# Rotary embedding of the attention on VectorE in quarters of the partitions, and a sum of squares issued behind the cross attention's transposes

## The reference

```python
def _apply_rope(t, cos, sin):
    half = DIFF_HEAD_DIM // 2            # 32
    tf = t.astype(jnp.float32)
    t1, t2 = tf[..., :half], tf[..., half:]
    ...
    return jnp.concatenate([t1 * c - t2 * s, t1 * s + t2 * c], axis=-1)

q = _apply_rope(dq.reshape(Bsz, S, DIFF_HEADS, 2, DIFF_HEAD_DIM), cos, sin)
k = _apply_rope(dk.reshape(Bsz, S, DIFF_HEADS, 2, DIFF_HEAD_DIM), cos, sin)
v = dv.reshape(Bsz, S, DIFF_HEADS, 2 * DIFF_HEAD_DIM)
o = _diff_attention(q, k, v, lam)
o = _rmsnorm(o, diff_norm_w[layer]) * (1.0 - lambda_init)
y_diff = o.reshape(Bsz, S, DIFF_WIDTH) * jax.nn.silu(dg.astype(jnp.float32))
```

## Time and profile before

| what | value |
|---|---|
| median of 3 runs | 2605.24 us (2599.07 to 2606.93) |
| the profiled execution | 2600.93 us |
| its span, first to last instruction | 2599.1 us |
| TensorE products busy | 2454.3 us, 94% |
| VectorE busy | 1722.5 us, 66% |
| ScalarE busy | 1349.6 us, 52% |
| mean granted clock of TensorE | 0.986 of full speed |

### The profile page before, as it was taken

How to read it: one execution, slowest core, us unless ns; L and a number is a source line. 1 busy time by engine, 2 the same in 40 slices (tenths; PEclk the granted TensorE clock), 3 DMA queues, 4 the chain that set the end, 5 groups by cost and what they waited for, 6 DMA issues and landing times.

```text
span 2599.1 us, 51367 instructions
## 1 busy us (share of the span) xinstructions
PE 2454.3 (94%) x18962; PEld 2341.4 (90%) x18962; DVE 1722.5 (66%) x2571; ACT 1349.6 (52%) x2376; POOL 88.9 (3%) x96
## 2 busy tenths in 40 slices
PE   5898899999989989999999999999999999999998
PEld 4788799999978878999999999799999999889998
DVE  4677776666767776667576567577657656667655
ACT  4677655553457774555344444544445435555443
POOL 0000000000000000000010001001001001001000
PEclk9999999999989999999999999999999999999999
DMA  5344444445434444443545545344554554434553
GB/s 155 114 130 131 130 130 146 146 129 169 141 112 132 131 130 130 134 153 104 193 146 181 171 150 175 93 146 146 177 173 152 178 167 150 139 103 143 181 170 106
DMA packets 397711, 376.16 MB, mean 145 GB/s; under 512 B 27822, under 2 KB 396382, under 8 KB 397422
## 3 DMA queue, kind: packets, MB, share of 16 engines
q1 hardware_dynamic: 397550, 373.94, 45.5%
HBM read 372.84 MB, written 1.05 MB: 144 GB/s over the span
## 4 chain that ended last, share of the span: by engine, by line
PE 66%; issue 23%; DVE 5%; ACT 3%; POOLq 2%; DVEq 1%; DMA 1%; POOL 0%; SPq 0%; ACTq 0%
PE ps L501 18%; PE ps L503 18%; PE ps L502 18%; POOLq L466 1%; PE ps L715 1%; PE ps L716 1%; PE ps L717 1%; ACT scratch L960 1%; ACT w_hi L960 1%; DVE w_lo L1396 1%; DMA raw<-in_ffn_w_up 1%; PE ps L741 1%; DVE xT L1502 1%; PE ps L729 1%; PE ps L772 1%
## 5 line engine op out<-in xcount | busy, mean ns | idle before, releaser
L1396 DVE TENSOR_TENSOR w_lo<-raw,w_hi 128x1024 fp32r<-128x1024 f32 x704 | 860.7, 1229 | 471.4 <-ACT w_hi L960 469.3
L501 PE MATMUL ps<-x_hi,w_hi 128*128 128x272 f32 (+1 forms) x3648 | 1060.1, 291 | 22.3 <-DVE w_lo L1396 14.4
L502 PE MATMUL ps<-x_lo,w_hi 128*128 128x272 f32 (+1 forms) x3648 | 1043.8, 286 | 0.0
L503 PE MATMUL ps<-x_hi,w_lo 128*128 128x272 f32 (+1 forms) x3648 | 1042.2, 286 | 0.0
L960 ACT ACTIVATE w_hi<-raw 128x1024 fp32r<-128x1024 f32 x704 | 736.2, 1054 | 512.2 <-PE ps L503 358.3
L501 PEld LDWEIGHTS ps<-x_hi,w_hi 128*128 128x128 f32 x3648 | 690.9, 189 | 51.4 <-issue 25.9
L502 PEld LDWEIGHTS ps<-x_lo,w_hi 128*128 128x128 f32 x3648 | 692.6, 190 | 2.1
L503 PEld LDWEIGHTS ps<-x_hi,w_lo 128*128 128x128 f32 x3648 | 693.2, 190 | 0.0
L501 PE MATMUL ps<-big_r,w_hi 128*128 128x272 f32 x832 | 240.7, 289 | 0.0
L503 PE MATMUL ps<-big_r,w_lo 128*128 128x272 f32 x832 | 240.0, 289 | 0.0
L960 ACT ACTIVATE scratch<-ps 128x256 f32<-128x256 f32 (+9 forms) x328 | 122.6, 385 | 190.7 <-PE ps L717 88.7
(11 more groups left out here) (285 smaller groups left out, 3073.1 us busy)
## 6 DMA issues: line engine op xcount, KB each, us to landing
raw<-in_w_in SPq DMA_DIRECT2D x224, 512.0 KB, 4.6
raw<-in_ffn_w_up SPq DMA_DIRECT2D x176, 512.0 KB, 4.4
raw<-in_ffn_w_down SPq DMA_DIRECT2D x64, 512.0 KB, 4.3
raw<-in_mix_w_in SPq DMA_DIRECT2D x64, 512.0 KB, 4.6
raw<-in_w_mem_kv SPq DMA_DIRECT2D x32, 512.0 KB, 4.3
raw<-in_w_br_ssd SPq DMA_DIRECT2D x32, 512.0 KB, 4.2
raw<-in_ffn_w_down SPq DMA_DIRECT2D x32, 384.0 KB, 3.4
raw<-in_w_br_diff SPq DMA_DIRECT2D x16, 512.0 KB, 3.9
```

The costliest lines, as they stand in the source:

```text
L501: mm(out, wh, xh, start=first, stop=False)
L502: mm(out, wh, xl, start=False, stop=False)
L503: return mm(out, wl, xh, start=False, stop=last)
L1396: tt(w_lo[:, p % PARTS, :, :], raw[:, p // 2 % RAW, :, (p % 2) * P:(p % 2 + 1) * P], wh_f[:, p % PARTS, :, :], ALU.subtract).then_inc(lo_r ...
```

## The change

1. The rotation products of TensorE, their constant and their semaphore go, and with them TensorE's waits for `att_ready` and for tiles 2 and 3.
2. VectorE rotates alone, in two calls of `rope(k)`, one for the queries and one for the keys: one product with the cosines on 128 partitions, four products with the sines on 32 partitions each, which read from the neighbouring quarter of the partitions, a drain, and one addition. All have 2 x 256 elements. The sign of the sine now comes from the constant `K_INV`.
3. The calls stand behind the splits of parts 5 and 6, not behind that of part 7.
4. In the first three passes the sum of squares is issued behind the four transposes of the cross attention, in the last one ahead of them as before.

```diff
-    c[:, K_ROT:K_ROT + P] = rot(0, DIFF_DIM, P)
...
-    c[:, K_INV] = inv[np.arange(P) % (DIFF_DIM // 2)]
+    c[:, K_INV] = inv[np.arange(P) % (DIFF_DIM // 2)] * np.where(np.arange(P) % DIFF_DIM < DIFF_DIM // 2, 1, -1)
...
                     token_tile(4, 4, 0, x1)
-                    pe.wait_ge(S["att_ready"], N + 1)
-                    read(T, 2)
-                    read(T, 3)
-                    for n in range(4):
-                        mm(ps[2 + n // 2][:, (n % 2) * SEQ:(n % 2 + 1) * SEQ], const[:, K_ROT:K_ROT + P], qk_raw[:, n, :],
-                           start=True, stop=True).then_inc(S["rot_done"], 1)
                     token_tile(5, 4, 1, x1)
                     proj(Q, T, 6, 6, x1)
...
-                    pe.wait_ge(S["qk_ready"], N * 4 + 4)
+                    pe.wait_ge(S["qk_ready"], N * 2 + 2)
...
-                    pe.wait_ge(S["o_squared"], N + 1)
-                    mm(ps[3][:, :], ones, o_sq, start=True, stop=True).then_inc(S["osum_done"], 1)
+                    def o_sum():
+                        pe.wait_ge(S["o_squared"], N + 1)
+                        mm(ps[3][:, :], ones, o_sq, start=True, stop=True).then_inc(S["osum_done"], 1)
+
+                    if i == 3:
+                        o_sum()
                     pe.wait_ge(S["cn_ready"], N + 1)
                     for t in range(2):
                         for kt in range(2):
                             m = pe.transpose(ps[5][:, kt * SEQ + t * P:kt * SEQ + (t + 1) * P], pc[:, t, kt * P:(kt + 1) * P], ident)
                     m.then_inc(S["cturned"], 1)
+                    if i < 3:
+                        o_sum()
...
+                    def rope(k):
+
+                        read(T, 2 * k)
+                        read(T, 2 * k + 1)
+                        two = slice(2 * k, 2 * k + 2)
+                        tt(qk[:, two, :], qk_raw[:, two, :], wide(cosT[:, :], 2), ALU.mult)
+                        for to in range(0, P, DIFF_DIM // 2):
+                            of = to + DIFF_DIM // 2 if to % DIFF_DIM == 0 else to - DIFF_DIM // 2
+                            to_rows, of_rows = slice(to, to + DIFF_DIM // 2), slice(of, of + DIFF_DIM // 2)
+                            tt(rope_t[to_rows, :, :], qk_raw[of_rows, two, :], wide(sinT[of_rows, :], 2), ALU.mult)
+                        v.drain()
+                        tt(qk[:, two, :], qk[:, two, :], rope_t, ALU.add).then_inc(S["qk_ready"], 1)
+                        v.drain()
+
                     for p in range(4, 8):
                         split(Q, p)
-                    for n in range(4):
-                        v.drain()
-                        v.wait_ge(S["rot_done"], N * 4 + 2 * (n // 2) + 2)
-                        tt(rope_t[:, 0, :], ps[2 + n // 2][:, (n % 2) * SEQ:(n % 2 + 1) * SEQ], sinT[:, :], ALU.mult)
-                        tt(rope_t[:, 1, :], qk_raw[:, n, :], cosT[:, :], ALU.mult)
-                        v.drain()
-                        tt(qk[:, n, :], rope_t[:, 0, :], rope_t[:, 1, :], ALU.add).then_inc(S["qk_ready"], 1)
+                        if p in (5, 6):
+                            rope(p - 5)
                     for p in range(8, 11):
                         split(Q, p)
```

## The result

The changed kernel takes 2622.02 us (median of 4 runs, 2620.23 to 2625.22), the kernel before 2603.05 us on the same chip (4 runs, 2599.07 to 2606.93). The forecast was 10.2 us more. The direction and the chain of waits came out as forecast, the size did not. The profiled execution took 2625.22 us, with a span of 2623.4. One execution further down, of the kernel with the sum of squares alone, took 3380.29 us at a granted clock of 0.657 and is left out of its ratio.

The account below looks back on a forecast made before the run. TensorE was taken to bound the kernel. Per layer, three later passes lose 0.62 us each and the first 3.26: 2 x (3 x 0.62 + 3.26) = 10.2 us more on 2605.24, so 2615 us, range 2601 to 2623.

Parts of the forecast that it names:

- The bound and the saving: Attention loop: TensorE sets the pace; removing its rotation products saves 1.66 us a pass, 13.3 us in all.
- The cost of a call: VectorE's rotation: one call takes 4.44 us, its sine products starting 0.705 us apart.
- Rival 1: VectorE's rotation: moves between quarters are free, a call takes 4.06 us; 2607 us, 2609 with clock fall; chance 0.2.
- The chain through unit 5: Later passes: late split 7 delays unit 5's load, ScalarE's split 10 and tile 10; 0.62 us lost each.
- The sum of squares: Cross attention: moving it behind the transposes gains 0 to 0.1 us in each of six passes, counted as nothing.
- So I expect a fall here, and none in the later passes: Before tile 9: clock falls only after first passes' 3.42 us gap, tile 9 takes 4.40 us, loss 3.26.
- Rival 4: Later passes, tile 9: clock also falls after the 2.12 us gap, each loses 1.96; 18.3 more, 2623 us; chance 0.08.
- A load takes 4.95 us from its first issue: Unit 5's load: 4.95 us from first issue to the ScalarE split that waits for it, used for all passes.

## Why the prediction was right and where it failed

**The bound and the saving: right.** TensorE's queue sets the pace, and the rotation products are worth 1.66 us a pass: with the load in time a pass is 1.80 us shorter.

**The cost of a call: right.** 4.40 us against 4.44; 0.70 between sine products against 0.705. Rival 1 (free moves between quarters, 0.61 us apart) is refuted by the 0.70; even with the crossing taken out, the time was 1.0053 of before.

**The chain through unit 5: right, and shown from three sides.** The load left 11.1 us behind unit 4 (forecast about 11), ScalarE waited 4.28 us for it (forecast some 4), TensorE stood 2.03 us before tile 9 (forecast 2.12), and the second passes grew by 0.65 and 0.79 us (forecast 0.62). Moving the one call off the load's path removes it all; moving both calls off makes the rotated tensors late instead; the late load alone, without any rotation on VectorE's side, makes the same wait.

**The sum of squares: right.** The wait before the last product went from 0.69 to 0.61 us, inside the bounds of 0 to 0.1; the part alone is 1.0000 of before.

**"So I expect a fall here, and none in the later passes": wrong.** This is one of the two mis-sized terms. The clock fell in the third pass of both layers, behind gaps of 2.15 and 3.02 us, for 2.13 and 2.99 us more where 0.62 each was forecast. The step went from one row, a gap of 2.22 us with a usual first product behind it, to "no fall at that length". The first product is no evidence: at 477.65 it also takes its usual 0.38 us, and the tile behind it 4.06. And the same gap in layer 2 of the same trace would have told against the step (TensorE's timeline, and the windows behind both gaps of 2.22 us):

```profile
1217.46 0.36 PE L501 MATMUL ps<-scratch_r,w_hi 128*128 128x256 f32 x1 [2.22 <-DVE big_r L1755]
```
```profile
563.40:567.80 4.40, 4.37 (x36) 4.40 (x37) 4.40 (x5) 4.37 (x5) 0.00 (x0) 1.00 0.00 2
1217.40:1221.80 4.40, 4.34 (x24) 4.37 (x25) 4.40 (x5) 4.40 (x5) 0.00 (x0) 0.61 0.00 0
```

The first products are alike, 0.36 us, but in layer 2 the clock is 0.61 and 24 products take 4.43 us instead of 2.94. In the twelve traces the clock fell behind 18 of the 24 gaps at this place, all of 2.21 to 2.23 us.

Rival 4 (a fall in all six later passes) was priced at 1.96 us a pass, where 2.13 and 2.99 were measured, and occurred in two of six. In the first passes the fall was expected, but sized at 4.40 us for tile 9 by the row of one pass: 5.00 and 5.28 were measured, 1.5 us more in the two layers. The trace of the kernel before had the other value too. In the first pass of layer 2 the gap before tile 4 is the same, but the clock behind it 0.50 and not 0.62 (TensorE's timeline and window; tile 4 is followed by the rotation products):

```profile
986.90 0.58 PE L715 MATMUL ps<-w_hi,x_hi 128*128 128x256 f32 x1 [3.27 <-DVE w_lo L1396]
...
992.19 2.14 PE L729 MATMUL ps<-scratch,const 128*128 128x256 f32 x8
```
```profile
986.90:991.30 4.40, 4.40 (x20) 4.40 (x21) 2.22 (x2) 0.00 (x0) 0.00 (x0) 0.50 0.69 237
```

There tile 4 took 992.19 - 986.90 = 5.29 us, not 4.40.

**"A load takes 4.95 us from its first issue": wrong in the first passes.** It was one row's value and stood without a range. In the second pass it held (5.02). In the first passes the loads took 5.88 and 7.58 us and the gaps were 4.31 and 4.82 us instead of 3.42, 2.3 us more in the two layers. (In layer 2 the load was 2.63 us too long and the gap only 1.40, since tiles 4 to 8 took 1.2 us more than in layer 1, 19.31 against 18.11, at the low clock behind the gap before tile 4.) In the third pass of layer 2 the load took 6.01 us and the gap 3.02. Why these loads are long is argued above and not shown.

Those terms put the miss together, gap and clock. First passes: 0.89 + 0.60 for layer 1 and 1.40 + 0.88 for layer 2, 3.8 us, which is all of theirs. Third passes: the gaps were 0.03 and 0.90 us longer than the forecast 2.12, and the rest of their miss of 1.51 and 2.37, about 1.5 us each, is the fall, 3.9 together. The remaining 0.4 us are spread over the four others. In all that is some 4.4 us of clock, beyond the 3 that the forecast had for it, and 3.2 of late loads.

**What was luck.** The time of 2622.02 us lies inside the stated range of 2601 to 2623, at its very edge. That upper end was rival 4's, a fall in all six later passes, and the time came out there by two falls, larger falls in the first passes and long loads instead. And the forecast of 2615 us stood on a median of 2605.24 for the kernel before; on 2603.05 the same sum would have said 2613.

**What stays open.** Which of the later gaps is followed by a fall isn't settled: of equal gaps of 2.75 us half were. With unit 6 held back, all later gaps were 2.0 us, the second pass of layer 1 had the fall (59.84 us long) and the five others none. And why the load is long in the first passes is open, as told above. The medians differ by 19.0 us and the loops of the two profiled executions by 18.4; the spans differ by 24.3, of which 2.1 lie ahead of the first loop, 1.9 between the two and 1.9 behind the second. That is work that the change doesn't touch, and I count it as difference between executions: 1.4 of the 1.9 between the loops is the gap of 2.22 us behind the first loop, which has a fall in the trace after (24 products in 4.37 us) and none in the one before (2.94), and over all the traces the stretch between the loops varies from 429.0 to 432.9 us and the one behind from 1387.0 to 1393.6.

## What to carry to other kernels

Work that moves to an engine with slack delays everything that this engine releases: ask of each of its later instructions which transfer or buffer waits for its semaphore, and put the new work behind the last release that is urgent and ahead of the first use of its result; here one place in the order of one call was worth 30 us. Where a forecast leaves a gap before TensorE, price it with the fall of the clock as a chance, not as none: its cost was 1.0 to 2.2 us on the tile behind the gap, and the gap's length didn't tell which. A duration that stands at the head of a chain, and the price of a fall too, deserve several rows, not one: in the trace of the kernel before, layer 2 alone would have corrected both of the rows on the clock that were taken from layer 1.

## What the runs showed of the hardware

Gaps of one length before TensorE are not all followed by the same clock. The clock fell behind one of five gaps of 1.96 to 2.15 us before tile 9 in the changed kernel, one of six of 1.96 to 2.02 us with unit 6 held back, two of four of 2.54 to 2.58 us with unit 5 late, and three of six of 2.75 us with both calls behind split 7. It fell behind 18 of 24 gaps of 2.21 to 2.23 us behind the loops, in all twelve traces together. Behind each gap of 2.8 us or more before tiles 4 and 9 it fell, in every trace. The depth differs too: behind the gap of 3.26 to 3.29 us before tile 4, in the first passes of the ten kernels that leave it empty, tile 4 took 4.25 to 4.42 us nine times and 5.29 us eleven times, where it takes 2.9 with the gap filled. Unused products in the gap kept the clock at 1.00 at the places tried (behind tile 8, and ahead of tile 4). Two of the three kernels with them were faster than the ones without by more than the intervals; on top of the moved rotation the gain was too small to tell.

A unit of 1 MB that takes 4.96 to 5.25 us from its first issue to its consumer in most passes took up to 8.09 us, in the longest case with a tail that moved mostly at 20 to 31 GB/s for some 3 us. Each time that an instruction packet began in the first 3.5 us of its way it took 5.76 us or more in the five traces counted; that the packet is the cause is not shown.
